# Two passes over the first tile of the mixing stages, and one branch over all further expert blocks, in a two-block float32 kernel

## What is computed

```python
# layer 1
mixed = concat([rmsnorm(out_a, g_out_a), rmsnorm(out_b, g_out_b)])   # two groups of 512 columns
x = x + mixed @ w_out
x = x + hierarchical_moe(rmsnorm(x, g_ffn_norm), ...)                # top 2 of 32 experts, blocks of 128 rows
# layer 2 and 3 (even and odd mixer)
ret = rms_norm(ret).reshape(B, S, 512) * silu(rg)                    # four heads of 128 columns
mix = concat([ret, sb * silu(sg)]);   y = mix @ even_w_out
hc = rms_norm(hc).reshape(B, S, 512) * silu(hg)                      # four heads of 128 columns
mix = concat([hc, hl * silu(lg)]);    y = mix @ odd_w_out
x = x + rms_norm(y, post_norm_w)
```

## Time and profile before

| | us |
|---|---|
| median of 3 runs | 2569.16 (2568.18 to 2571.93) |
| the profiled execution, whole | 2562.74 |
| its span, first to last instruction | 2560.8 |
| mean granted clock of TensorE | 0.921 of full |
| PE busy in the span | 2184.0 (85%) |
| DVE busy | 1300.5 (51%) |
| ACT busy | 1055.2 (41%) |
| POOL busy | 563.3 (22%) |

### The profile page before, as it was taken

One profiled execution on the slowest core, in us unless ns is written; L12 is line 12 of the kernel. 1 busy time (PEld: TensorE's weight loads), 2 busy tenths in 40 slices (PEclk: granted clock), 3 DMA queues, 4 the chain that ended last, 5 costly groups with the idle time before them and its releaser, 6 DMA issues. The chain is left out here.

```text
span 2560.8 us, 34305 instructions
## 1 busy us (share of the span) xinstructions
PE 2184.0 (85%) x12244; PEld 1806.9 (71%) x12244; DVE 1300.5 (51%) x2177; ACT 1055.2 (41%) x1924; POOL 563.3 (22%) x643
## 2 busy tenths in 40 slices
PE   6996997999887499999389999678778899956768
PEld 5885886999776366676268888578667778845657
DVE  3333675555454466666352120667665343427843
ACT  3332655555342155555252110256453333337631
POOL 1003101622011121231120000456432000017722
PEclk9998998999988699999689999889989899977879
DMA  4686866422153489998364221443162433141152
GB/s 154 206 239 184 242 221 163 119 62 53 34 199 118 178 305 371 356 347 324 140 231 152 78 83 50 128 92 77 43 229 84 153 138 117 62 139 42 43 189 91
DMA packets 216721, 399.16 MB, mean 156 GB/s; under 512 B 90512, under 2 KB 111376, under 8 KB 203904
## 3 DMA queue, kind: packets, MB, share of 16 engines
q1 hardware_dynamic: 177008, 314.52, 38.5%
q10 hardware_dynamic: 28384, 61.62, 6.3%
q0 software_dynamic: 11184, 21.13, 2.3%
HBM read 300.16 MB, written 114.85 MB: 162 GB/s over the span
## 5 line engine op out<-in xcount | busy, mean ns | idle before, releaser
L78 PE MATMUL pe_acc<-pe_w,hT 128*128 128x512 f32 x960 | 225.1, 396 | 5.3 <-DVE hT L722 5.3
L78 PEld LDWEIGHTS pe_acc<-pe_w,hT 128*128 128x128 f32 x960 | 183.5, 192 | 44.0 <-DVE hT L722 5.7
L78 PE MATMUL ex_gu<-hT,ex_xT 128*128 128x512 f32 x792 | 194.4, 401 | 0.8 <-DVE hT L2382 0.8
L2382 DVE TENSOR_TENSOR hT<-ex_raw,hT 128x2048 fp32r<-128x2048 f32 x66 | 150.8, 2287 | 86.8 <-ACT hT L2353 82.7
L78 PE MATMUL pg_acc<-hT,pg_w 128*128 128x512 f32 x768 | 179.4, 395 | 9.1 <-DVE pg_w L263 9.1
L78 PEld LDWEIGHTS pg_acc<-hT,pg_w 128*128 128x128 f32 x768 | 145.1, 189 | 42.4 <-DVE pg_w L263 9.5
L78 PEld LDWEIGHTS ex_gu<-hT,ex_xT 128*128 128x128 f32 x792 | 147.5, 190 | 34.5 <-DVE hT L2382 1.2
L2353 ACT ACTIVATE hT<-ex_raw 128x2048 fp32r<-128x2048 f32 x66 | 126.2, 1913 | 40.8 <-PEq L47 23.9
L302 DVE COPY pe_o<-pe_acc 128x512 f32<-128x512 f32 x28 | 19.3, 691 | 206.7 <-PE pe_acc L78 206.7
L1757 PE MATMUL ab_op<-ab_v,ab_pT 128*128 128x64 f32 x1024 | 121.3, 272 | 0.0
L2311 PE MATMUL ex_dn<-ex_wd,ex_hT 128*128 128x512 f32 x264 | 118.7, 592 | 0.8 <-ACT ex_hT L2347 0.8
(11 more groups left out here) (480 smaller groups left out, 5009.1 us busy)
## 6 DMA issues: line engine op xcount, KB each, us to landing
ex_raw<-in_w_gate SPq DMA_DIRECT2D x33, 1024.0 KB, 7.3
ex_raw<-in_w_up SPq DMA_DIRECT2D x33, 1024.0 KB, 11.1
ex_wd<-in_w_down SPq DMA_DIRECT2D x33, 1024.0 KB, 14.0
pe_raw<-in_even_w_in SPq DMA_DIRECT2D x6, 2048.0 KB, 8.4
pg_raw<-in_odd_w_in SPq DMA_DIRECT2D x5, 2048.0 KB, 10.3
scr_q<-pa_o SPq DMA_DIRECT2D x32, 256.0 KB, 4.1
scr_k<-pa_o SPq DMA_DIRECT2D x32, 256.0 KB, 3.8
hT<-scr_k SPq DMA_DIRECT2D x16, 512.0 KB, 6.7
```

The source lines that it names most:

```text
L78: mm = pe.matmul(out, a(p, k), b(q, k), start=(k == 0 and i == 0), stop=(k == n - 1 and i == 2))
L2382: dve.tensor_tensor(split(s, LO)[:, :, g, :], raw[:, s % NW, g, :].rearrange("p (k n) -> p k n", k=8), split(s, HI)[:, :, g, :].bitcast(F3 ...
```

## The change

1. `pool_x` makes the means of all groups of a tile with one instruction instead of one each. All groups of a stage have one width. Stages with one group are as they were.
2. `first_tile` takes the place of the two halves of tile 0 on PE. Pass 1 has, for each piece, HI and LO of the rows against HI of the weight, both halves of columns (32 matmuls), and waits for `hi` alone. Then come the transposes of tile 1, and pass 2 with HI of the rows against LO of the weight (16 matmuls), which waits for `lo`. Later tiles use `product` with the same order as before.
3. On ACT the copy of tile 0 stands behind 2, 4 and 6 pieces of `hi` (am, em, om) instead of 6; the squares of tile 1 stand before pieces 6 and 7 instead of behind them. On DVE `dve_z` of tile 0 is first, `dve_turn` of tile 0 comes after two pieces of `lo`, and `dve_z` of tile 1 before the last two. On SP the loads of tile 1 in am stand before pieces 6 and 7; in em and om they stood there already.
4. `further` has one branch, taken if n is at most 1, over 14 bodies written in a row.

```diff
@@ pool_x
-            for n, (c0, w) in enumerate(self.groups):
-                pool.tensor_scalar(self.ms[:, u, n:n + 1], self.ss[:, u, n:n + 1], 1.0 / w, EPS, ALU.mult,
-                                   ALU.add).then_inc(self.ms_ok, 1)
-            pool.wait_ge(self.ms_ok, self.ng * (t + 1))
+            pool.tensor_scalar(self.ms[:, u, 0:self.ng], self.ss[:, u, 0:self.ng], 1.0 / self.groups[0][1], EPS, ALU.mult,
+                               ALU.add).then_inc(self.ms_ok, 1)
+            pool.wait_ge(self.ms_ok, t + 1)
@@ mix_out
+        early = 6 if order[0] else 4 if f.gate else 2
...
-                    if i == NR:
+                    if i == 6:
                         f.load(sp, 1)
...
-                if NR == 8:
-                    f.load(sp, 1)
...
-                hi(0, 6)
+                hi(0, early)
                 f.act_turn(act, 0)
+                hi(early, 6)
+                f.act_x(act, 1)
                 hi(6, 8)
-                f.act_x(act, 1)
...
+                f.dve_z(dve, 0)
                 if gain is not None:
                     dve.wait_ge(gain_in, 16 * len(gain))
                 lo(0, 2)
-                f.dve_z(dve, 0)
-                lo(2, 5)
                 f.dve_turn(dve, 0)
-                lo(5, 8)
+                lo(2, 6)
+                f.dve_z(dve, 1)
+                lo(6, 8)
...
+                def first_tile(pe):
                     for i, k in enumerate(order):
-                        if first:
-                            if k == 0:
-                                f.pe_turn(pe, 0)
-                                pe.wait_ge(f.lo_ok, 1)
-                            pe.wait_ge(lo_ok, i + 1)
...
+                        if k == 0:
+                            f.pe_turn(pe, 0)
+                            pe.wait_ge(f.lo_ok, 1)
+                        pe.wait_ge(hi_ok, i + 1)
+                        for p in (HI, LO):
+                            for nn in (slice(0, BANK), slice(BANK, D)):
+                                pe.matmul(acc[0][:, nn], hT[:, p, k, 0:P], w[:, HI, k, nn], start=(i == 0 and p == HI), stop=False)
+                    f.pe_turn(pe, 1)
+                    for i, k in enumerate(order):
+                        pe.wait_ge(lo_ok, i + 1)
+                        for nn in (slice(0, BANK), slice(BANK, D)):
+                            mm = pe.matmul(acc[0][:, nn], hT[:, HI, k, 0:P], w[:, LO, k, nn], start=False, stop=(i == 7))
+                    mm.then_inc(y_done, 1)
...
-                half(pe, 0, 0, True)
-                f.pe_turn(pe, 1)
-                half(pe, 0, 1, False).then_inc(y_done, 1)
@@ experts
-            with eng.Fori(0, (NOV - 1) // 2) as r:
-                with eng.If(n > r * 2 + 1):
-                    for i in range(2):
-                        body(r * 2 + (i + 1))
+            with eng.If(n > 1):
+                for j in range(1, NOV):
+                    body(j)
```

17 lines of the change are left out of this document (8 added, 9 removed).

## The result

The changed kernel takes 2552.41 us in the median of 13 runs (2544.81 to 2562.11), the kernel before 2568.18 (2561.05 to 2580.09, 13 runs). The medians differ by 15.8 us. The ratio is 0.9937, with a 95% interval of 0.9919 to 0.9955: 16.2 us less, between 11.6 and 20.8. Forecast were 10.0 us less, and 2559.2 us with a range from 2554.0 to 2566.5: right direction, too small. The changed kernel was also run once more beside the experiments: 0.9941 (0.9921 to 0.9961), 15.2 us less.

The account below looks back on a forecast made before the run. PE's late starts behind tile scaling bound the mixing stages, POOL's loop and drain the experts' end. 3.9 - 1.4 + 3.6 + 3.9 = 10.0 us off gave a median of 2559.2 us, range 2554 to 2566.5.

Parts of the forecast that it names:

- am, 3.9: Stage am: scaling tile 0 first and a shorter chain bring the transposes of tile 2 nearer, gain 3.9 us.
- em, -1.4: Stage em: transposes of tile 2 1.0 us nearer, less 2.4 for a fallen clock, a net loss of 1.4 us.
- the chain to the first matmul loses three of four means and a little of DVE's queue: 0.8 to 1.2 us: Start of em, tile 0: the first matmul comes 0.8 to 1.2 us nearer.
- em's clock, 2.4: In em, PE idles 3.8 us, the clock falls, and tile 1's 48 matmuls pay 2.4 us, a cold start's price.
- Rival C: In em the clock stays up despite PE's idle: gain 12.4 us, whole 2556.8; chance 0.18.
- om, 3.6: Stage om: transposes of tile 2 come 3.0 to 4.5 us nearer, taken as a gain of 3.6 us.
- Rival D: The clock falls once more, in the idle before tile 2 of om or am: gain 7.6 us, 2561.6; chance 0.20.
- Experts, 3.9: End of the experts: one branch replaces POOL's loop, so its drain starts earlier and lasts as long, gain 3.9 us.
- Rival A: End of the experts: the drain has its own end, experts give 0: gain 6.1 us, 2563.1; chance 0.15.
- Rival B: Experts: the branch over 14 bodies finds its target not loaded, costing 3.8 us: gain 6.2, 2563.0; chance 0.08.
- Rival E: All three mixing stages: PE never warms in tile 0, pass 1 over 13 us, whole slower at 2575; chance 0.05.
- The other Rows stages at nothing: Means in the other Rows stages are unchanged, so those stages gain nothing.

Follow-up runs that it names:

- order alone: Kernel before with only the new order of work on SP, ACT and DVE; PE, four means and loop as before: ratio 1.0004 (0.9988 to 1.002).
- filler: Kernel before with extra matmuls into the unused accumulator where PE waited in om and em: ratio 0.9983 (0.9965 to 1.0001).
- mean alone: Kernel before with only the one mean instruction for all groups of a tile: ratio 0.9963 (0.9948 to 0.9979).

## Why the prediction was too small

- **am, 3.9**: 4.2 measured. Start and the chain to tile 2 as forecast, pass 1 in 8.9 to 10.3 us (9.8).
- **em, -1.4**: 2.7 shorter. The step that failed first is "the chain to the first matmul loses three of four means and a little of DVE's queue: 0.8 to 1.2 us". "Scaling and LO of tile 0 already stood first where it mattered", the prediction says, and they didn't. DVE's queue was not a little: the scaling stood behind two pieces of lo, and moving those is worth some 2 us before the mean is counted. The rows for this lay in the trace of before (the scaling at 1862.95 starts 0.17 after POOL's power, and right behind DVE's own work); I read the wait for POOL as the only one, and POOL's 4.0 us there as its own time (2.0 with no lo beside it, order alone). This made the transposes of tile 1 2.6 us nearer (29.7 in the mean of two, 27.1 of three) where I had 0.2. The 8.2 us from there to tile 2 (8.3 forecast) and the idle of 3.5 (3.8) were right.
- **em's clock, 2.4**: the second term that was off. The clock fell in all three executions, as forecast, but the price was 1.6, 1.6 and 0.8. I took the price of a cold start for that of a fall in an idle stretch. And I charged it to the change alone, though the code of before, with its 2.49 us of idle, pays 1.6 too in one of two executions (11.18 and 12.80). Rival C, that the clock stays, fell. Taking means over the executions, the transposes of tile 2 came 3.5 us nearer (forecast 1.0) and the 48 matmuls cost 0.5 more (forecast 2.4): of the 4.1 us by which em was missed, the first step holds 2.5 and the clock 1.9, less 0.3 elsewhere in the stage. That only half of before's executions pay is the luck in it: the profiled pair alone, before without the fall and the changed kernel with it, shows 1.4.
- **om, 3.6**: 4.4. The transposes of tile 1 as forecast within 1.2 us (24.0 and 23.5 behind the start, forecast 24.7); pass 2 with its transposes was put at 8.0, half clock, "as it was there before", but took 5.9 in both executions (5.3 and 5.5 the pass alone). The clock there was low since PE had idled for 2.96 us in the stretch that the change shortens (2.6 now; filler there kept it up). Rival D, one more fall, didn't come in om or am.
- **Experts, 3.9**: 3.7, and 4.0 from the last matmul on. Rival A fell: the drain lasted 5.46 in all five executions with the loop and 5.5 in all twelve with the branch. Rival B fell: POOL's branch over 14 bodies took 58 ns and the gap behind it 0.44 us, against the 3.8 that it had put there. By the 108 ns that Advanced Engine Details and Errata, Control Flow Timing, in the Trainium skill gives for a compare-and-branch, the gain would have been 1.3, an estimate; 4.0 was measured. (The prediction put the whole at 2561.4 by it; its own terms give 2561.8.)
- **Rival E** fell: pass 1 took 8.9 to 10.3 us in am and em, not over 13, so the clock rose within it each time.
- **The other Rows stages at nothing**: no stage shows otherwise.
- **The reference point**: I set the forecast against the median of three runs, 2569.16; of thirteen it was 2568.18, which is 1.0 of the 6.8 us by which the median was missed. The rest is the sum: 5.0 by the stages, 5.8 by this median.

What stays open: the mean alone measured 9.5 us (5.4 to 13.4), its stages 4.5 in the one execution profiled. Its whole was expected at 1 to 2.5 us. Whether the remainder is its six runs or clock falls that it avoids in more executions than one profile can show was not settled.

## What to carry to other kernels

When the first product of a stage waits for a scaled tile, list what stands ahead of the scaling on its own engine, as well as whom it waits for; here both ended within 0.3 us of each other, and shortening the chain on POOL gave nothing (mean alone), freeing DVE's queue gave 2.3 of the 3.0 us (order alone), also because POOL ran faster once DVE was quiet, and both gave all. Price a wait of PE with the clock that may be lost behind it, here 0.8 to 2.4 us on 24 to 48 matmuls: two chains shortened by 0.8 us each were worth 1.7 to 3.5 up to tile 2 of om, one shortened by 2.0 was worth 0.4 at most, since the loss moved to the next wait. Matmuls into an unused accumulator kept the clock up behind the wait that they filled, if sized to end before the wait does; in om of the changed kernel the loss moved to the next wait then too.
